# Adding the two column halves on TensorE, and a new split of the turned weights between VectorE and ScalarE

## The reference

```python
s = einsum('nbqgrd,nbkgd->ngrbqk', qb, kb) * hd ** -0.5
s = where(mask, s + bias, -inf)
m = max(s, -1);  m = maximum(m, sk)        # sk: sinks, kind c alone
p = exp(s - m[..., None]);  den = sum(p, -1) (+ exp(sk - m))
o = einsum('ngrbqk,nbkgd->nbqgrd', p, vb);  o = o / den
...
o_cmp = einsum('ngrtc,ncgd->ntgrd', p_cmp, vc)          # 127 compressed keys
o = g[0] * o_cmp + g[1] * o_slc + g[2] * o_win          # gates, heads of kind a
```

## Time and profile before

| | before |
|---|---|
| median of 3 runs | 3151.39 us (3147.83 to 3151.8) |
| profiled execution, its own time | 3153.93 us |
| its span, first to last instruction | 3152.2 us |
| attention, k and b stretch | 723 to 1005 us |
| attention, c stretch | 1005 to 1100 us |
| attention, w and s stretch | 1100 to 1590 us |
| PE busy, share of the span | 3048.0 us, 97% |
| DVE busy, share of the span | 2063.1 us, 65% |
| mean granted TensorE clock | 0.993 |

### The profile page before, as it was taken

One profiled execution on the slowest core, in us unless ns is written; L12 is line 12 of the kernel. 1 busy time (PEld: TensorE's weight loads), 2 busy tenths in 40 slices (PEclk: granted clock), 3 DMA queues, 4 the chain that ended last, 5 costly groups with the idle time before them and its releaser, 6 DMA issues. The chain is left out here.

```text
span 3152.2 us, 44863 instructions
## 1 busy us (share of the span) xinstructions
PE 3048.0 (97%) x16138; PEld 2482.5 (79%) x16138; DVE 2063.1 (65%) x3931; ACT 1468.7 (47%) x2657; POOL 1202.5 (38%) x840
## 2 busy tenths in 40 slices
PE   8999999999888999999999999999999999999998
PEld 8888888887767766766678778888888788888887
DVE  5565565556768977877744687777555477777343
ACT  5332443236767866666633444444434344444332
POOL 2444244310000024442110198888110688885010
PEclk9999999999999999999999999999999999999999
DMA  4464545376666623431144522221565222223553
GB/s 142 163 187 144 176 156 172 124 209 224 240 222 240 184 69 83 134 89 43 61 114 126 170 87 81 90 84 67 187 218 186 97 83 92 81 80 113 185 196 107
DMA packets 274811, 433.90 MB, mean 138 GB/s; under 512 B 125760, under 2 KB 178240, under 8 KB 261568
## 3 DMA queue, kind: packets, MB, share of 16 engines
q1 hardware_dynamic: 265600, 395.70, 38.1%
q0 software_dynamic: 8992, 35.33, 3.4%
HBM read 312.51 MB, written 126.84 MB: 139 GB/s over the span
## 5 line engine op out<-in xcount | busy, mean ns | idle before, releaser
L1111 PE MATMUL z_banks<-ops,z_area 128*128 128x512 f32 x1720 | 434.1, 391 | 3.2 <-DVE z_area L858 3.2
L3194 PE MATMUL f_banks<-f_wt 128*128 128x512 f32 x1776 | 406.1, 389 | 0.0
L3194 PEld LDWEIGHTS f_banks<-f_wt 128*128 128x128 f32 x1776 | 333.3, 188 | 69.2
L1111 PEld LDWEIGHTS z_banks<-ops,z_area 128*128 128x128 f32 x1720 | 322.9, 188 | 70.3 <-DVE z_area L858 3.6
L2564 POOL TENSOR_TENSOR f_wt<-f_wt_f,f_wt 128x1024 fp32r<-128x1024 f32 x132 | 316.1, 2418 | 64.6 <-ACT f_wt L2695 59.1
L2043 ACT ACTIVATE w_small<-w_small,a_stats 128x128 f32<-128x128 f32 (+3 forms) x510 | 256.2, 516 | 90.5 <-DVE a_stats L2128 63.2
L3165 PE MATMUL f_banks<-low,f_wt 128*128 128x512 f32 x704 | 274.0, 389 | 0.0
L2986 DVE SCALAR_TENSOR_TENSOR near<-w_small,vk,near 128x1024 f32<-128x1024 f32 x88 | 231.2, 2628 | 1.7
L2128 DVE CUSTOM_DVE_ANT_0 w_small<-a_s_ps,near 128x128 f32<-128x128 f32 (+2 forms) x456 | 164.5, 392 | 89.2 <-PE a_s_ps L1929 79.1
L1973 PE MATMUL a_ot_ps<-a_turned_w,vs 128*64 128x256 f32 (+3 forms) x1452 | 221.3, 428 | 0.0
L3165 PE MATMUL f_banks<-f_oo,f_wt 128*128 128x512 f32 x704 | 217.0, 390 | 2.5 <-ACT kc_f L2729 1.2
(11 more groups left out here) (306 smaller groups left out, 7079.4 us busy)
## 6 DMA issues: line engine op xcount, KB each, us to landing
low<-z_parts SPq DMA_DIRECT2D x46, 1024.0 KB, 6.2
f_wt_f<-in_w_ffn SPq DMA_DIRECT2D x74, 512.0 KB, 4.1
z_area_f<-in_w_z SPq DMA_DIRECT2D x54, 512.0 KB, 5.1
f_raw_f<-in_w_ffn SPq DMA_DIRECT2D x22, 1024.0 KB, 4.8
f_wt_f<-in_w_ffn SPq DMA_DIRECT2D x22, 1024.0 KB, 5.3
g_up<-near SPq DMA_DIRECT2D x44, 512.0 KB, 2.6
f_wt_f<-g_up SPq DMA_DIRECT2D x88, 256.0 KB, 4.3
z_parts<-z_st_hi SPq DMA_DIRECT2D x68, 256.0 KB, 2.3
```

The costliest lines, as they stand in the source:

```text
L1111: last = pe.matmul(banks[:, bank, :], w[:, c * P:(c + 1) * P], rows[:, c * 512:(c + 1) * 512], start=(first and c == 0 and q == 0), stop=( ...
L3194: last = pe.matmul(banks[:, 2 * t + n, :], g[:, tok], w[:, n, :], start=(d == 0 and x == 0), stop=(d == NF - 1 and x == 2))
```

## The change

Three things are altered, all in `attend`. First, for all kinds but k, `turn_out` no longer turns 128 columns; it multiplies the same 128x128 piece of `ot` by `both`, two 64x64 identities one above the other, which turns and adds the halves at once and gives 64 columns a tile. This is an ordinary 32-bit matmul in place of a transpose. Second, VectorE's and POOL's finishing work has one half to read: a copy in place of the reduction in kind b, no reduction in kind c, a multiplication of half the width in w and s, one addition in place of two on POOL. Third, in units of kinds b and c a batch goes to ScalarE where `b % 3` is 0 and to VectorE otherwise; k, w, s and the batches of the choice keep `b % 2`.

```diff
-        batch["eng"] = b % 2
-        counts[b % 2] += 1
-        batch["count"] = counts[b % 2]
+        batch["eng"] = min(b % 3, 1) if batch["u"] is not None and kind[batch["u"] // 4] in "bc" else b % 2
+        counts[batch["eng"]] += 1
+        batch["count"] = counts[batch["eng"]]
...
-        add = sb("add", [P, 4, 2 * HD])
+        add = sb("add", [P, 4, HD])
+        both = sb("both", [P, HD])
...
+        on_sum = on_ps[:].rearrange("p i q -> p (i q)")[:, 0:4 * HD].rearrange("p (i d) -> p i d", d=HD)
...
-                pool.tensor_tensor(rows, rows, add[:, :, 0:HD], ALU.add).then_inc(upper_added, 1)
-                pool.wait_ge(upper_added, g - late + 1)
-                pool.tensor_tensor(rows, rows, add[:, :, HD:2 * HD], ALU.add).then_inc(out_done, 1)
+                pool.tensor_tensor(rows, rows, add[:], ALU.add).then_inc(out_done, 1)
...
-                for i in range(4):
-                    last = pe.transpose(on_ps[:, i, 0:w], ot[0:w, i * P:(i + 1) * P], idt[0:w, 0:w])
+                if kind[g // 4] == "k":
+                    for i in range(4):
+                        last = pe.transpose(on_ps[:, i, 0:w], ot[0:w, i * P:(i + 1) * P], idt[0:w, 0:w])
+                else:
+                    pe.wait_ge(both_set, 2)
+                    for i in range(4):
+                        last = pe.matmul(on_sum[:, i, :], ot[:, i * P:(i + 1) * P], both[:], start=True, stop=True)
...
+            for half in (slice(0, HD), slice(HD, P)):
+                dve.tensor_copy(both[half, :], idt[half, half]).then_inc(both_set, 1)
...
-                    dve.tensor_reduce(rows[:, :, 0:HD], halves, AX.X, ALU.add).then_inc(out_done, 1)
+                    dve.tensor_copy(rows[:, :, 0:HD], on_sum).then_inc(out_done, 1)
...
-                    dve.tensor_reduce(rows[:, :, 0:HD], halves, AX.X, ALU.add).then_inc(chain, 1)
+                    dve.wait_ge(chain, at + 1)
+                    dve.reciprocal(coef[:], coef[:]).then_inc(chain, 1)
                     dve.wait_ge(chain, at + 2)
-                    dve.reciprocal(coef[:], coef[:]).then_inc(chain, 1)
-                    dve.wait_ge(chain, at + 3)
-                    dve.tensor_tensor(rows[:, :, 0:HD], rows[:, :, 0:HD], coef[:].unsqueeze(2).to_broadcast([P, 4, HD]),
+                    dve.tensor_tensor(rows[:, :, 0:HD], on_sum, coef[:].unsqueeze(2).to_broadcast([P, 4, HD]),
...
-                    dve.tensor_tensor(add[:], on_ps[:], coef[:].unsqueeze(2).to_broadcast([P, 4, 2 * HD]),
+                    dve.tensor_tensor(add[:], on_sum, coef[:].unsqueeze(2).to_broadcast([P, 4, HD]),
```

More of the change, by code:

```diff
@@ L1582, in attend @@
     pick_batch = {batch["pick"]: b for b, batch in enumerate(batches) if "pick" in batch}
-    steps = {"b": 1, "c": 3, "w": 2, "s": 2, "k": 5}
+    steps = {"b": 1, "c": 2, "w": 2, "s": 2, "k": 5}
     sums = [0]
@@ L1654, in attend @@
         blank_set = sem("blank_set")
-        upper_added = sem("upper_added")
+        both_set = sem("both_set")
         scored = sem("scored")
@@ L2136, in finish @@
                 u, on, at32 = g // 4, on_ps[:, :, 0:HD + 1], (4 * g) % 32
-                halves = on_ps[:].rearrange("p i (h d) -> p i d h", h=2)
                 den = stats[:, at32:at32 + 4, 0:1]
```

## The result

The changed kernel takes 3204.4 us (4 runs, 3202.43 to 3205.8) beside 3150.65 us for the kernel before on the same chips: a ratio of 1.0172, 95% interval 1.016 to 1.0184. It is 54 us slower; forecast were 32, with 54.2 as the first rival, "PE's whole price shows".

A forecast was written before the change was run, and what follows sets the result against it. PE was taken to bound w and s, PE and DVE nearly full in c, a ring of waits in k and b. Terms 16 + 12 + 4 = +32 us on 3151.4 gave 3183 us, range 3158 to 3207.

The forecast's parts named there:

- PE's whole price shows: Rival: turning out always stands on the path, all 54.2 us count and DVE's savings are hidden, 3206 us; chance 0.15.
- The instruction: Turning out: the 32-bit matmul runs as two load and multiply pairs, 0.89 us a group, 0.45 more than now.
- the estimate that the prediction made from it: Turning out: four passes of 64 columns cost what the old transposes do, 0.44 us a group, so no PE term.
- The path: Attention stretches: how much of PE's 54.2 us lengthens the run, +16 in w and s, +12 in b, +4 in c.
- I take 5 or 6 us off: +16: w and s stretch: of PE's 21.7 us more, 5 or 6 go into idle time, leaving +16 us.
- I choose 0.25 a group: Kind b: each group costs 0.25 us, between bounds 0 (all swallowed) and 21.7 us, +12 us in all.
- 0.17 a group: c stretch: each group costs 0.17 us, between DVE's +0.04 and PE's +0.45, +4 us in all.
- VectorE's relief: Finishing in b, c, w and s: shorter DVE work, 26.3 us less in all after the new split's additions.
- The batches: New split in b and c: DVE gets 9.3 and 5.8 us more, ACT 7.9 and 4.9 us less.
- The rings swallow it: Rival: PE's idle in k, b and c takes the 32.5 us, only w and s show, about 3160 us; chance 0.13.
- The turn costs no more than now: Rival: the new turn is no dearer, only DVE's and ACT's relief is left, -12 us, 3139; chance 0.06.
- DVE is what holds b and c: Rival: b and c gain 13.5 us by shorter finishes, w and s mostly idle-covered, -12 us, 3139; chance 0.06.

The follow-up runs named there:

- e6: Changed kernel with a moving operand of 128 columns (double identity twice, side by side), finishing reads the first 64; +57.7 us against the kernel before.
- e3: Changed kernel with turned output and double identity in the one-pass 32-bit format (F32R), new split kept; +4.6 us against the kernel before.
- e7: Changed kernel with the one-pass 32-bit turn and the old batch split (b % 2 everywhere); -6.4 us against the kernel before.
- e1: Changed kernel with the batches split as before (b % 2 everywhere), new turn and finishing kept; +50.8 us against the kernel before.
- e4: Changed kernel with the old 128-column transposes and old split, so the lighter finishing alone, second half never added; -6.4 us against the kernel before.
- e5: Kernel before with the four transposes of the turning out issued twice for all kinds but k; +50.3 us against the kernel before.
- e8: Kernel before with b and c batches split the other way, ScalarE two of three, VectorE one; +7.1 us against the kernel before.
- e10: e7 with VectorE and ScalarE swapped in the alternation of b and c units; +10.3 us against the kernel before.
- e11: e7 with b and c batches that close at a group's last tile on VectorE, all others on ScalarE; -6.6 us against the kernel before.
- e12: Kernel before with b and c batches that close at a group's last tile on VectorE, all others on ScalarE; +2.5 us against the kernel before.
- e2: Kernel before with the new split of the batches alone; +8.4 us against the kernel before.

## Why the prediction was right or wrong

**The instruction, right.** A 32-bit matmul that is no transpose runs as two load and multiply pairs. The twin at line 1325 gave the count (960 records); its own step was 0.118 us, and the 0.111 came from the warm starts of the scores. The Trainium skill, "FP8 and Floating Point Precision", TensorE Precision Notes, has four passes for true FP32; the estimate that the prediction made from it was 0.44 us a group. That does not give the time here: 0.44 would have added nothing, and the traces add 0.45. At 128 columns (e6) the same estimate would be 0.87 us a group and near what the trace shows, but the time is the same at 64. With the one-pass format (e3, e7) it falls by half. The price was forecast at 0.45 us a group, 54.2 us in all; the distances to the next instruction show 54 us, and e1 less e4 57 us.

**The path, wrong in size, and this is what the forecast of 32 us got wrong:** "I take 5 or 6 us off: +16" in w and s, "Bounds 0 ... and 21.7; I choose 0.25 a group" in b, "0.17 a group" in c. The new finishing and the turn together, with the old split (e1), gave 22.6, 18.9 and 7.9 us where I had 16, 12 and 4 (for b and c with the split in). I had read PE's idle time as room that more PE work could fill, and said that some of it shrinks because the other engines get ahead. e5 shows that it isn't room: 52.3 us of added transposes, with nothing else changed, cost 50.3. PE's idle time in w and s is 20 us in both kernels, and its two largest waits there have not shrunk at all. In the changed kernel they are, against 8.3 and 5.2 us in the earlier trace rows:

```profile
PE a_t_ps L1940 <- ACT a_turned_w L2037: 8.3, 13, 1.7
PE a_t_ps L1940 <- DVE a_turned_w L2037: 5.2, 13, 0.8
```

My reading of it is that these waits come after PE's own work in the same ring, so that a later PE makes VectorE and ScalarE later too, and the same wait is met again, only shifted. The whole w and s stretch lasted 513.7 us where I looked for 506, k, b and c together 412.4 where I looked for 393.

**VectorE's relief, wrong in size.** The sum for b counted its shorter finish at 0.27 us a group on the ring, and in c I let 0.684 us speak. Alone (e4) it is worth 1.2, 2.6 and 0.3 us in the three stretches of the profiled executions, and 6.4 us by the medians. The forecast of 32 so had two errors with one sign: too much of PE's price hidden, too much of VectorE's gain seen.

**The batches, wrong in kind.** I priced them by amounts, 15 us more on VectorE and 13 less on ScalarE. e8 lowers VectorE's amount and loses as much; e10 nearly leaves the amounts and loses twice as much. So it counts which engine takes which batch, apart from the amounts. What about the batch decides, its place in the group's order or something that goes with it, is not shown, since the direct test (e11, e12) brought no gain. In the changed kernel the new split is worth some 3 us (changed less e1, not clear of noise), on the kernel before 8.4; that PE's longer turn hides the rest is a guess.

**The rivals.** "PE's whole price shows", given 0.15, was what happened. That its 54.2 us meet the measured 53.8 so closely is partly luck: VectorE's savings are not wholly hidden (6.4 us, e4), and the split and the turn's size make up for them. The forecast's range ended at 3207, just above that rival's 3206, and the measured 3204.4 lies in it by the rival's path and not by the forecast's. "The rings swallow it" is refuted by e5, where k, b and c paid 30.3 of 31.4 us. "The turn costs no more than now" describes e7, not this kernel. "DVE is what holds b and c" is refuted by e4: of 29.4 us less work of VectorE in b and c, 3.8 us came back.

What stays open: by what way the split costs its time, and which units carry it. That e3 and e7 lie 11 us apart and e2 8.4 us from the kernel before is no question, since 3 us are within the noise.

## What to carry to other kernels

Before an addition or a move is folded into a 32-bit matmul, look in the trace for a matmul of that kind and count its records against the program: a transpose is one load and multiply pair, an ordinary 32-bit matmul is two. With a full set of weights each pair cost 0.11 us here, at 64 columns as at 128; with 512 columns (line 1973 in the earlier trace rows) the two starts lie 0.43 us apart, so there the columns count. Idle time on the fullest engine of a ring was not room for more work of that engine: added time counted nearly one for one (50.3 of 52.3 us), removed time for three quarters (18.2 of 24.4), and relief of the second engine for a seventh (6.4 of 42). When copies are dealt to engines that run in program order, their lengths alone did not foretell the time here (e8, e10); look also at what stands behind each copy while it waits.

## What the runs showed of the hardware

The one-pass 32-bit format has weight loads as long as those of the ordinary one (192 ns against 192) and half as many pairs (480 for 960), so that its gain at this place goes with the number of pairs. And 128 columns in place of 64 (e6) cost 4 us over 960 pairs, at most a few ns each and not clear of the noise.
